# One core, Strassen-form SwiGLU: when ScalarE, VectorE and GpSimd prepare the operands on entry and between two phases

## The reference, cut to what matters

```python
def rmsnorm(x, g):
    return x * rsqrt(mean(x * x, axis=-1, keepdims=True) + EPS) * g
x = x + g2[:, None, :] * y                       # y: attention output @ w_out
h = rmsnorm(x, ffn2_norm) * (1 + sc3[:, None, :]) + sh3[:, None, :]
x = x + 0.5 * g3[:, None, :] * ((silu(h @ wg) * (h @ wu)) @ wd)
x = rmsnorm(x, final_norm)
```

## Time and profile before

| what | value |
|---|---|
| time, median of 3 runs | 3146.11 us (3145.6 to 3149.04) |
| time of the profiled execution | 3152.61 us |
| its span, first to last instruction | 3150.7 us |
| PE busy | 3020.5 us, 96% of the span |
| DVE, ACT, POOL busy | 1667.9, 1193.6, 1361.6 us |
| mean granted clock of TensorE | 0.983 |
| HBM read and written | 262 MB, 83 GB/s over the span |

### The profile page before, as it was taken

One profiled execution on the slowest core, in us unless ns is written; L12 is line 12 of the kernel. 1 busy time (PEld: TensorE's weight loads), 2 busy tenths in 40 slices (PEclk: granted clock), 3 DMA queues, 4 the chain that ended last, 5 costly groups with the idle time before them and its releaser, 6 DMA issues.

```text
span 3150.7 us, 45626 instructions
## 1 busy us (share of the span) xinstructions
PE 3020.5 (96%) x15385; PEld 2608.0 (83%) x15385; DVE 1667.9 (53%) x3010; ACT 1193.6 (38%) x2026; POOL 1361.6 (43%) x765
## 2 busy tenths in 40 slices
PE   7999999999999988997989999989999998999998
PEld 3888888888888867885656667979999998999998
DVE  5576667766672346886544332353433456434435
ACT  6311111111111135775767775443333343333334
POOL 0111111111111143333646666666666666666673
PEclk9999999999999999998999999989999999999999
DMA  7121212212121023556413225422222121222222
GB/s 268 39 69 52 65 55 80 68 52 63 57 75 34 27 81 119 146 141 163 121 54 83 74 77 160 119 74 67 67 80 67 60 74 41 81 67 67 67 80 100
DMA packets 341520, 262.50 MB, mean 83 GB/s; under 512 B 19771, under 2 KB 309934, under 8 KB 341422
## 3 DMA queue, kind: packets, MB, share of 16 engines
q1 hardware_dynamic: 341422, 261.21, 28.2%
HBM read 215.71 MB, written 45.45 MB: 83 GB/s over the span
## 4 chain that ended last, share of the span: by engine, by line
PE 40%; POOL 9%; issue 6%; DVE 4%; ACT 2%; SPq 1%; DMA 0%; DVEq 0%; POOLq 0%; ACTq 0%
POOL XT_r L1967 8%; PE PS L2671 6%; PE PS L2672 6%; PE PS L2673 6%; PE PS L518 6%; PE PS L519 6%; PE PS L520 6%; POOL W_lo L2416 0%; DVE SL L2327 0%; PE PS L1666 0%; DVE XT L2177 0%; ACT SLf L2303 0%; PE PS L772 0%; ACT z_sb L1184 0%; POOL W_lo L2116 0%
## 5 line engine op out<-in xcount | busy, mean ns | idle before, releaser
L512 POOL TENSOR_TENSOR W_lo<-raw,W_hi 128x1024 fp32r<-128x1024 f32 x66 | 158.7, 2411 | 959.0 <-ACT W_hi L480 959.0
L518 PE MATMUL PS<-H_hi,W_hi 128*128 128x512 f32 (+1 forms) x1312 | 500.3, 381 | 1.9 <-DVE H_lo L1921 1.4
L519 PE MATMUL PS<-H_lo,W_hi 128*128 128x512 f32 (+1 forms) x1312 | 497.0, 379 | 0.0
L520 PE MATMUL PS<-H_hi,W_lo 128*128 128x512 f32 (+1 forms) x1312 | 496.9, 379 | 0.0
L2416 POOL TENSOR_TENSOR W_lo<-quart,W_hi 128x1024 fp32r<-128x1024 f32 x132 | 320.4, 2436 | 263.5 <-ACT W_hi L2412 263.5
L2671 PE MATMUL PS<-SL,W_hi 128*128 128x384 f32 x1056 | 356.6, 338 | 20.8 <-POOL W_lo L2416 19.8
L1967 POOL TENSOR_TENSOR XT_r<-XT,XT_r 128x512 fp32r<-128x512 f32 x224 | 287.0, 1287 | 181.7 <-ACT XT_r L1819 181.1
L2672 PE MATMUL PS<-SL,W_hi 128*128 128x384 f32 x1056 | 355.4, 337 | 0.0
L2673 PE MATMUL PS<-SL,W_lo 128*128 128x384 f32 x1056 | 355.0, 336 | 0.0
L2177 DVE SCALAR_TENSOR_TENSOR XT<-PS,mod,XT 128x384 f32<-128x384 f32 (+1 forms) x480 | 243.2, 534 | 186.2 <-PE PS L520 186.2
L480 ACT ACTIVATE W_hi<-raw 128x1024 fp32r<-128x1024 f32 x66 | 68.6, 1055 | 604.2 <-PE PS L520 604.2
(11 more groups left out here) (294 smaller groups left out, 6291.0 us busy)
## 6 DMA issues: line engine op xcount, KB each, us to landing
ada_r<-in_ada_w SPq DMA_DIRECT2D x192, 128.0 KB, 2.3
quart<-in_ffn_wg SPq DMA_DIRECT2D x88, 256.0 KB, 3.9
quart<-in_ffn_wu SPq DMA_DIRECT2D x88, 256.0 KB, 4.1
down<-in_ffn_wd SPq DMA_DIRECT2D x44, 512.0 KB, 3.5
raw<-in_w_out SPq DMA_DIRECT2D x30, 512.0 KB, 3.7
ada_w_sb<-in_ada_w SPq DMA_DIRECT2D x6, 2048.0 KB, 15.8
raw<-in_ffn_wg SPq DMA_DIRECT2D x22, 512.0 KB, 4.1
raw<-in_ffn_wu SPq DMA_DIRECT2D x22, 512.0 KB, 4.5
```

Source lines behind the costliest of these rows:

```text
L512: pool.tensor_tensor(W_lo[:, n % WS, :], raw[:, n % RS, :], W_hi[:, n % WS, :].bitcast(F32), ALU.subtract).then_inc(w_ready, 1)
L518: pe.matmul(out, w_hi, m_hi, start=first, stop=False)
L519: pe.matmul(out, w_hi, m_lo, start=False, stop=False)
L520: return pe.matmul(out, w_lo, m_hi, start=False, stop=last)
```

## The change

ACT on entry splits the weights of units 0, 1 and 2 before it touches T3, and takes the high parts of T4 and B22 between the first copies of round 0. At the start of round 11 only T2 stands ahead of the copies, and T3, T4, B22 follow unit 3. The operand B11 of phase two is scaled (DVE, after the 8th down unit's add) and shifted (ACT, at the round's end) in round 0, into four rows of SL (12 to 15 of the fourth column) that are free by then; its high part is taken in round 10 after hidden part 0. In round 10 the shift of B21 and unit 8 stand before the silus, and the shift of B12 comes after the next round's unit 0. The sums of squares of block 3 move by two products: PE runs them after T2 and T3 instead of after B21 and T1, POOL's pair sums stand after low parts 4 and 5, the root after copy 5, and the two reciprocals after hidden part 3.

```diff
@@ -2274,5 +2274,10 @@
 
-        def raw_row(j, kp):
+        EDGE = NWC - 1
+
+        def raw_row(h, j, kp):
             kb, nb = RAW_AT[j]
-            return SLf[:, KD * kb + 4 + kp, nb, :]
+            return SLf[:, 12 + kp, EDGE, :] if h == 1 and j == B11 else SLf[:, KD * kb + 4 + kp, nb, :]
+
+        def raw4(h, j):
+            return SLf[:, 12:16, EDGE, :] if h == 1 and j == B11 else operand4(SLf, X4f, j, 1)
 
@@ -2282,5 +2287,7 @@
             c = 2 * h + nb
-            dve.wait_ge(rstd_ready, 2 * NCH + (2 if h == 0 and nb == 0 else 3 if h == 0 else NWC + 1) - 1)
+            dve.wait_ge(rstd_ready, 2 * NCH + 2 * h + nb + 1)
             if h == 0:
                 dve.wait_ge(wo_done, (1 + nb) * KD)
+            elif j == B11:
+                dve.wait_ge(sq_used, 2 + (2 * NCH + NWC) * NPP)
             else:
@@ -2291,3 +2298,3 @@
                     cut = slice(a - c * NB, b - c * NB)
-                    mm = dve.scalar_tensor_tensor(out=raw_row(j, kp)[:, cut], in0=XT[:, k, a:b], scalar=hscale[:, 2, k, s:s + 1],
+                    mm = dve.scalar_tensor_tensor(out=raw_row(h, j, kp)[:, cut], in0=XT[:, k, a:b], scalar=hscale[:, 2, k, s:s + 1],
                                                   in1=(rstd_a, rstd_b)[h][:, nb, cut], op0=ALU.mult, op1=ALU.mult)
@@ -2301,3 +2308,3 @@
                 for a, b, s in column_spans(c * NB, (c + 1) * NB):
-                    row = raw_row(j, kp)[:, a - c * NB:b - c * NB]
+                    row = raw_row(h, j, kp)[:, a - c * NB:b - c * NB]
                     mm = act.activation(row, row, ACT.Identity, bias=mod[:, SH3 * KD + 4 * kb + kp, s:s + 1])
@@ -2314,3 +2321,3 @@
             a, b = OP_T[j]
-            dve.tensor_tensor(operand4(SLf, X4f, j, 1), operand4(SLf, X4f, a, 1), operand4(SLf, X4f, b, 1), ALU.subtract) \
+            dve.tensor_tensor(operand4(SLf, X4f, j, 1), raw4(h, a), raw4(h, b), ALU.subtract) \
                .then_inc(op_x, 1)
@@ -2322,3 +2329,5 @@
                 act.wait_ge(op_shift, h * 2 * KD + SHIFT_NO[j] + 4)
-            act.activation(operand4(SL, X4, j, 0), operand4(SLf, X4f, j, 1), ACT.Copy).then_inc(op_hi, 1)
+            if h == 1 and j == B11:
+                act.wait_ge(st_steps, st_at(NR - 1, product_step(B11, 1)))
+            act.activation(operand4(SL, X4, j, 0), raw4(h, j), ACT.Copy).then_inc(op_hi, 1)
 
@@ -2326,3 +2335,3 @@
             dve.wait_ge(op_hi, OPH0 + h * PN + j + 1)
-            dve.tensor_tensor(operand4(SL, X4, j, 1), operand4(SLf, X4f, j, 1), operand4(SL, X4, j, 0).bitcast(F32), ALU.subtract) \
+            dve.tensor_tensor(operand4(SL, X4, j, 1), raw4(h, j), operand4(SL, X4, j, 0).bitcast(F32), ALU.subtract) \
                .then_inc(op_ready, 1)
@@ -2442,4 +2451,2 @@
                     st_lo_pool(pool, R, u)
-                if is_round(R, 0):
-                    pair_up(pool, 2, NWC - 1)
                 st_sum(pool, R, 3)
@@ -2447,2 +2454,4 @@
                     st_lo_pool(pool, R, u)
+                    if is_round(R, 0) and u in (4, 5):
+                        pair_up(pool, 2, NWC - 1, u - 4)
                 if not is_round(R, 2 * NR - 1):
@@ -2467,3 +2476,2 @@
         DOWN_BANKS = (6, 7, 0, 1, 2, 3, 4, 5)
-        EDGE = NWC - 1
         HOME_1, HOME_E = 8, 10
@@ -2506,12 +2514,18 @@
             def body(R, h):
+                turns = is_round(R, NR - 1)
                 if not is_round(R, 0):
                     st_hi_act(act, R, 1)
-                st_hi_act(act, R, 2)
+                    st_hi_act(act, R, 2)
                 if is_round(R, NR):
-                    for j in (T2, T3, T4, B22):
-                        op_hi_act(act, 1, j)
+                    op_hi_act(act, 1, T2)
                 part_keep_act(act, R, 0)
                 part_keep_act(act, R, 1)
+                if is_round(R, 0):
+                    op_hi_act(act, 0, T4)
                 st_hi_act(act, R, 3)
+                if is_round(R, NR):
+                    for j in (T3, T4, B22):
+                        op_hi_act(act, 1, j)
                 if is_round(R, 0):
+                    op_hi_act(act, 0, B22)
                     sums_act(act, 2, NWC - 1, (0, 4))
@@ -2522,9 +2536,7 @@
                     sums_act(act, 2, NWC - 1, (4, KD))
+                if turns:
+                    op_hi_act(act, 1, B11)
                 st_hi_act(act, R, 5)
-                if is_round(R, 0):
-                    root_act(act, 2, NWC - 1)
                 part_keep_act(act, R, 2)
                 part_keep_act(act, R, 3)
-                if is_round(R, NR - 1):
-                    op_shift_act(act, 1, B11)
                 st_hi_act(act, R, 6)
@@ -2532,6 +2544,8 @@
                 part_keep_act(act, R, 5)
-                if is_round(R, NR - 1):
-                    op_shift_act(act, 1, B21)
-                    op_hi_act(act, 1, B11)
+                if is_round(R, 0):
+                    root_act(act, 2, NWC - 1)
                 st_hi_act(act, R, 7)
+                if turns:
+                    op_shift_act(act, 1, B21)
+                    st_hi_act(act, R, 8)
                 st_silu_act(act, R, 1)
@@ -2539,21 +2553,22 @@
                 st_silu_act(act, R, 2)
-                if is_round(R, NR - 1):
-                    op_shift_act(act, 1, B12)
-                st_hi_act(act, R, 8)
+                if not turns:
+                    st_hi_act(act, R, 8)
                 st_hid_act(act, R, 2)
-                if is_round(R, NR - 1):
+                if turns:
                     op_hi_act(act, 1, B21)
+                    st_hi_act(act, R, 0, 1)
+                    op_shift_act(act, 1, B12)
                 st_silu_act(act, R, 3)
                 st_hid_act(act, R, 3)
-                if is_round(R, NR - 1):
+                if is_round(R, 0):
+                    op_shift_act(act, 1, B11)
+                if turns:
                     op_hi_act(act, 1, T1)
                     op_shift_act(act, 1, B22)
-                if not is_round(R, 2 * NR - 1):
+                elif not is_round(R, 2 * NR - 1):
                     st_hi_act(act, R, 0, 1)
 
-            st_hi_act(act, 0, 0)
+            for u in range(WS):
+                st_hi_act(act, 0, u)
             op_hi_act(act, 0, T3)
-            op_hi_act(act, 0, T4)
-            st_hi_act(act, 0, 1)
-            op_hi_act(act, 0, B22)
             st_rounds(act, body)
@@ -2609,7 +2624,4 @@
                 if turns:
-                    op_x_dve(dve, 1, B11)
+                    op_lo_dve(dve, 1, B11)
                     op_x_dve(dve, 1, B21)
-                if is_round(R, 0):
-                    root_dve(dve, 2, NWC - 2)
-                    root_dve(dve, 2, NWC - 1)
                 st_add_dve(dve, R, 1)
@@ -2625,2 +2637,5 @@
                 st_hidden_dve(dve, R, 3)
+                if is_round(R, 0):
+                    root_dve(dve, 2, NWC - 2)
+                    root_dve(dve, 2, NWC - 1)
                 if turns:
@@ -2629,10 +2644,10 @@
                     st_down_dve(dve, R, h, i)
+                    if is_round(R, 0) and i == 7:
+                        op_x_dve(dve, 1, B11)
                     if turns:
                         if i == 3:
-                            op_lo_dve(dve, 1, B11)
-                        if i == 6:
                             op_t_dve(dve, 1, T2)
-                        if i == 9:
+                        if i == 7:
                             op_t_dve(dve, 1, T4)
-                        if i == 12:
+                        if i == 11:
                             op_lo_dve(dve, 1, B21)
@@ -2706,4 +2721,4 @@
                     st_product(pe, R, h, j)
-                    if is_round(R, 0) and j in (B21, T1):
-                        sums_pe(pe, 2, NWC - 1, j - B21)
+                    if is_round(R, 0) and j in (T2, T3):
+                        sums_pe(pe, 2, NWC - 1, j - T2)
                 st_down(pe, R, h)
```

More of the change, by code:

```diff
@@ L2532, in body @@
                 part_keep_act(act, R, 5)
-                if is_round(R, NR - 1):
+                if is_round(R, 0):
+                    root_act(act, 2, NWC - 1)
+                st_hi_act(act, R, 7)
+                if turns:
                     op_shift_act(act, 1, B21)
-                    op_hi_act(act, 1, B11)
-                st_hi_act(act, R, 7)
+                    st_hi_act(act, R, 8)
                 st_silu_act(act, R, 1)
@@ L2539, in body @@
                 st_silu_act(act, R, 2)
-                if is_round(R, NR - 1):
+                if not turns:
+                    st_hi_act(act, R, 8)
+                st_hid_act(act, R, 2)
+                if turns:
+                    op_hi_act(act, 1, B21)
+                    st_hi_act(act, R, 0, 1)
                     op_shift_act(act, 1, B12)
-                st_hi_act(act, R, 8)
-                st_hid_act(act, R, 2)
-                if is_round(R, NR - 1):
-                    op_hi_act(act, 1, B21)
                 st_silu_act(act, R, 3)
                 st_hid_act(act, R, 3)
```

(12 more changed lines are left out.)

## The result

The changed kernel takes 3156.06 us (median of ten runs, 3151.17 to 3158.52), the kernel before 3148.16 us (ten runs, 3143.58 to 3151.21): a ratio of 1.0025, with a 95% interval of 1.0016 to 1.0034. That is some 8 us slower, and above the forecast range; the bound of 0.2% lies within the interval. The profiled execution took 3155.96 us, with a span of 3154.2; before it was 3152.61 and 3150.7. The mean granted clock is 0.982, before 0.983.

What follows compares the result with a forecast made beforehand. PE alone bounds steady rounds; at the phase change and entry its waits for POOL's low parts put some 43 us at stake. Entry gain 1.1 less phase loss 0.9 gave 0.2 us less: 3145.9 for 3146.1, range 3141 to 3150.

Steps and rivals of the forecast that it cites:

- Steps 1 and 2: Entry: unit 1 ahead of T3 removes the 8.21 us wait before B21; T1 then starts at 2095.4 after 11.0 us idle.
- rival of milder turns: Faster rival: POOL mostly goes through beside DVE, T1 starts at 2088.8; 3134 us, chance 0.31.
- the change does nothing: Rival: T3's operand or a quarter's landing, not ACT's order, sets the waits, which stay; 3146 us, chance 0.03.
- Step 3: Entry, block 3's sums two products later: T4 starts at 2112.3 instead of about 2120.0, a gain of 7.7 us.
- Step 4: Entry, root between copy 5 and unit 7: down starts at 2122.3 instead of 2128.4, a gain of 6.1 us.
- Step 5: End of round 0, phase two's B11 made there: PE waits 0.8 and 3.0 us; entry gain 0 to 2.2, taken 1.1.
- Steps 6 to 8: Phase change, rounds 10 and 11: a loss of 2.1 us, or a gain of 0.1 with another order; taken loss 0.9.
- step 6: Round 10: POOL's sum 0 falls between B12's four scalings on DVE; down starts at 2592.0 instead of 2592.60.
- the other order: Round 10: DVE gets all four B12 scalings through before POOL's sum 0; down 2.2 us earlier, phase change gains 0.1.
- step 8: Round 11: T2 gains 5.1 us, but T3 waits for copy 2 and ends at 2648.3, before at 2646.2.
- slower rival: Round 10's hidden part 3 ends late, PE waits at down units 6 and 8 with slow clock; 3153 us, chance 0.20.

Runs made afterwards that it cites:

- second execution: The changed kernel run once more with nothing edited; 3153.23 us, ratio 1.0016 to the kernel before.
- four such swaps: Late second squares, unit 0 before B11's shift, B12's shift before hidden 2, add 0 before T4 and B22, against the changed kernel; together 3135.22 us, ratio 0.9946.
- unit 0 first: In round 0 ACT splits unit 0 of round 1 before shifting B11, against the changed kernel; 3146.39 us, ratio 0.9993.

## Why the prediction was wrong

**Steps 1 and 2, right.** B21 follows B11 at once, and the wait before T1 is 10.04 us where 11.0 was worked out; counted from B11, T1 comes at 18.5 us and was put at 19.3. POOL's four steps took 3.91, 3.75, 3.73 and 3.86 us, 15.25 in all where 16.0 was worked out. The first of them:

```profile
2077.15 3.91 POOL L2446 TENSOR_TENSOR qsum<-quart 128x1024 f32<-128x1024 f32 x1
```

So the rival of milder turns fell, and the pace of whole instructions by turns held: the chain is DVE's operands as much as POOL's own work. That the change does nothing fell too, since the 8.21 us before B21 went.

**Step 3, the one that failed.** It put T4 at 2112.3, which is 36.2 us after B11, from POOL's chain alone (low 4 and the pair sums). It asked when the pair sums could be made, and took for granted that the second squares were there. They wait for slots that the moved sums free: 7.90 us on ACT, and 2.68 us on PE before T3, a wait that the sum put at nothing. T4 came at 40.6, or 38.4 in the second execution. With the squares moved too it came at 36.06. That this is step 3's number to 0.1 is in part luck: T1 came 0.8 us sooner than worked out, and from T1 to T4 it took 17.5 us instead of 16.9. The gain of 7.7 us was 3.3 to 5.5.

**Step 4, right in itself.** From T4 to down it had 10.0 us; it was 9.3, with a wait of 0.56. ACT:

```profile
2114.37 1.28 ACT L764 ACT_TABLE_LOAD   x1
2115.66 0.58 ACT L764 ACTIVATE rstd_b<-PS,eps_col 128x384 f32<-128x384 f32 x1
```

The root starts 1.29 us after the start of the table load. The Trainium skill (ScalarE: Activation LUTs, "What ACT_TABLE_LOAD costs") states a drain of some 1.38 us on top of the load; here too there is none.

**Step 5, right in its waits, too hopeful in its choice.** It had 0.8 and 3.0 us, and 2.2 of clock as an open point. The rows have 1.12 and 2.68, and the clock fell behind the second in both executions. ACT and DVE in that place (first execution):

```profile
2135.50 2.88 ACT L2310 ACTIVATE SLf<-SLf,mod 128x256 f32<-128x256 f32 x8 [10.26 <-DVE SLf L2299]
```

```profile
2125.74 4.95 DVE L779 RECIPROCAL rstd_b<-rstd_b 128x384 f32<-128x384 f32 x2
```

The middle was taken (1.1 of 0 to 2.2); the dear end came. Behind a step that was itself 1.5 to 3.7 us late, the gain on entry became a loss of 1.3 to 3.5.

**Steps 6 to 8, right in their working.** PE at the change of phase:

```profile
2593.06 0.66 PE L518 MATMUL PS<-hid,W_hi 128*128 128x384 f32 x1 [5.29 <-DVE hid L2604]
...
2601.50 0.44 PE L518 MATMUL PS<-hid,W_hi 128*128 128x384 f32 x1 [0.25 <-DVE hid L2604]
...
2606.04 0.45 PE L518 MATMUL PS<-hid,W_hi 128*128 128x384 f32 x1 [2.19 <-DVE XT L2177]
...
2631.53 0.69 PE L2686 MATMUL PS<-SL,W_hi 128*128 128x384 f32 x1 [2.80 <-POOL W_lo L2425]
...
2642.59 0.66 PE L2686 MATMUL PS<-SL,W_hi 128*128 128x384 f32 x1 [3.80 <-ACT SLf L2500]
```

On the scale of before (1.4 us less) down is at 2591.7 and was put at 2592.0, round 11 at 2614.7 and was put at 2614.0, T2 at 2630.1 and was put at 2630.6. The waits at units 6 and 8 are 0.25 and 2.19 against 0.3 and 2.5, and T3 waits for the copy behind add 0. These rows carry the order of step 6, with sum 0 between the scalings:

```profile
2586.77 4.56 DVE L2299 SCALAR_TENSOR_TENSOR SLf<-XT,mod,rstd_b 128x384 f32<-128x384 f32 x4
```

```profile
2587.20 2.65 POOL L2446 TENSOR_TENSOR qsum<-quart 128x1024 f32<-128x1024 f32 x1
```

Four scalings took 4.56 us beside the sum, before 2.49. The working gave a loss of 2.1 and the other order a gain of 0.1, and the text took 0.9. It was 2.1 (2.0 in the second execution). The other order never came in any of the nine executions in which it could.

**The sum.** The forecast was 0.2 us less. Add 1.5 to 3.7 for step 3, 0.85 for step 5 (1.1 for its choice, less 0.25 by which the times around it were off) and 1.2 for the choice in step 8: a loss of 3.3 to 5.6 us. That the whole time shows 5.0 to 7.9 leaves some 2 us open. The slower rival had nearly the measured time (6.7 us over before), by luck, since its way was another: it wanted 2.4 us at down unit 6, where 0.25 was found. The range was too narrow on that side, since it held no term for a wait in the moved sums.

## What to carry to other kernels

When a step is moved, list what it frees as well as what it needs: a buffer that comes free later holds the producer of its next contents, and with it everything behind that producer on its engine. Put on an in-order engine first what already has its inputs and is waited for, and last what waits for another engine: four such swaps, each worth 3 to 6.5 us in its stretch, made of a change that lost 0.2% one that wins 0.5%. And where the working gives one value and a hope gives another, forecast the working.

## What the runs showed of the hardware

The same wait is not always followed by the same clock. The changed kernel waited 2.68 us before T3 in both of its executions, behind T2 and the sums at full clock. Windows of PE's wait and of what follows it (busy time and instructions of PE, PEld, DVE, ACT, POOL, then the granted clock), first execution:

```profile
2101.80:2103.80 2.00, 2.00 (x13) 2.00 (x12) 0.00 (x0) 0.00 (x0) 1.20 (x2) 1.00 0.00 0
...
2105.10:2107.80 2.70, 0.04 (x1) 0.01 (x1) 0.00 (x0) 2.70 (x7) 0.42 (x1) 1.00 0.00 0
2107.80:2109.80 2.00, 1.98 (x9) 2.00 (x9) 0.00 (x0) 1.20 (x2) 2.00 (x2) 0.72 0.00 0
2109.80:2111.80 2.00, 2.00 (x8) 2.00 (x8) 0.00 (x0) 0.48 (x1) 2.00 (x3) 0.50 0.30 87
```

Second execution:

```profile
2099.00:2101.00 2.00, 2.00 (x13) 2.00 (x12) 0.00 (x0) 0.00 (x0) 1.80 (x2) 1.00 0.21 84
...
2102.30:2105.00 2.70, 0.04 (x1) 0.07 (x1) 0.00 (x0) 2.70 (x6) 0.48 (x1) 1.00 0.00 0
2105.00:2107.00 2.00, 2.00 (x12) 2.00 (x13) 0.00 (x0) 1.15 (x2) 2.00 (x2) 1.00 0.00 0
2107.00:2109.00 2.00, 2.00 (x13) 2.00 (x12) 0.00 (x0) 0.49 (x1) 2.00 (x3) 1.00 0.31 90
```

In the first the clock falls to 0.50, the level of 1.2 GHz, some time after the wait; in the second it stays at 1.00, that of 2.4 GHz. From T3 to T4 it takes 6.8 us in the first and 5.3 in the second. That is 1.6 of the 2.2 us between the two entry stretches. The other 0.6 lies at T1: behind the same wait of 10.04 us the granted clock is 0.50 in the first 4 us and 0.54 in the next 2, in the second execution 0.57 and then 1.00. The wait of 2.68 before B21 of round 1 went both ways as well: with the squares moved, the way from T4 of round 0 to T4 of round 1 took 1.6 us less behind waits of 1.10 and 2.68. So did the wait before down unit 8 of round 10: from there to round 11 it is 10.0 us behind a wait of 2.19, and 8.7 in "unit 0 first" behind one of 2.07 (granted clock in the 6 us behind the wait 0.70 to 0.74, and 1.00). What decides it was not tried. In these rows a wait of 2.1 to 2.7 us costs itself or itself and 1.3 to 1.6 us more, and of one execution's stretch some 2 us are chance.
